# Expert blocks of 121 slots instead of 128, and a gate function that reads the bank directly

## What is computed

```
def expert_block(args):
    xe, e = args
    gu = xe @ w_gate_up[e] + b_gate_up[e]
    gate, up = gu[:, :D_FF], gu[:, D_FF:]
    gate = jnp.minimum(gate, SWIGLU_LIMIT)
    up = jnp.clip(up, -SWIGLU_LIMIT, SWIGLU_LIMIT)
    h = gate * jax.nn.sigmoid(SWIGLU_ALPHA * gate) * (up + 1.0)
    return h @ w_down[e] + b_down[e]
```

## Time and profile before

| | |
|---|---|
| time, median of 3 runs | 1645.02 us (1643.68 to 1648.96) |
| the profiled execution | 1642.78 us, of which the span from first to last instruction is 1641.0 |
| TensorE busy | 1497.4 us, 91% |
| TensorE weight loads | 1177.5 us, 72%, beside the matmuls |
| VectorE busy | 1407.9 us, 86% |
| ScalarE busy | 1011.4 us, 62% |
| GpSimd busy | 156.7 us, 10% |
| granted TensorE clock, mean | 0.955 |
| moved by DMA | 471 MB, 287 GB/s |

### The profile page before, as it was taken

How to read it: one execution, slowest core, us unless ns; L and a number is a source line. 1 busy time by engine, 2 the same in 40 slices (tenths; PEclk the granted TensorE clock), 3 DMA queues, 4 the chain that set the end, 5 groups by cost and what they waited for, 6 DMA issues and landing times. The chain is left out here.

```text
span 1641.0 us, 22871 instructions
## 1 busy us (share of the span) xinstructions
PE 1497.4 (91%) x7059; PEld 1177.5 (72%) x7060; DVE 1407.9 (86%) x1927; ACT 1011.4 (62%) x1201; POOL 156.7 (10%) x196
## 2 busy tenths in 40 slices
PE   5979999939999999999999999999999999999540
PEld 4868753538888888878888888788888888888430
DVE  3964547669999999999999999999999999999538
ACT  4001131137777787777778777777787777777421
POOL 6370001000000000000000000000000000000000
PEclk9979999959999999999999999999999999999775
DMA  8400064127999899889898887888999888989206
GB/s 276 61 1 29 31 218 194 62 91 317 366 376 377 370 368 371 340 341 373 366 371 367 366 367 326 361 370 366 372 371 371 360 338 368 371 369 370 91 16 266
DMA packets 81955, 471.15 MB, mean 287 GB/s; under 512 B 15969, under 2 KB 16965, under 8 KB 64495
## 3 DMA queue, kind: packets, MB, share of 16 engines
q1 hardware_dynamic: 70526, 451.31, 68.6%
q0 software_dynamic: 11232, 19.46, 3.2%
q10 hardware_dynamic: 168, 0.04, 0.0%
HBM read 463.59 MB, written 23.04 MB: 297 GB/s over the span
## 5 line engine op out<-in xcount | busy, mean ns | idle before, releaser
L1463 DVE TENSOR_TENSOR w_lo<-ring_lo,w_hi 128x1024 fp32r<-128x1024 f32 x528 | 616.2, 1218 | 10.9 <-ACT w_hi L1304 5.2
L1304 ACT ACTIVATE w_hi<-ring_lo 128x1024 fp32r<-128x1024 f32 x528 | 537.1, 1056 | 74.0 <-PE bank L1388 55.9
L1388 PE MATMUL bank<-w_hi,x_hi 128*128 128x512 f32 x1056 | 340.2, 403 | 5.6 <-DVE w_lo L1463 3.4
L1388 PE MATMUL bank<-w_lo,x_hi 128*128 128x512 f32 x1056 | 327.6, 392 | 0.0
L1388 PE MATMUL bank<-w_hi,x_lo 128*128 128x512 f32 x1056 | 326.3, 390 | 0.0
L1463 DVE TENSOR_TENSOR w_lo<-w_out,w_hi 128x1024 fp32r<-128x1024 f32 x264 | 310.7, 1218 | 6.2 <-ACT w_hi L1304 6.2
L1304 ACT ACTIVATE w_hi<-w_out 128x1024 fp32r<-128x1024 f32 x264 | 267.1, 1050 | 9.2 <-PE bank L1388 9.2
L1388 PEld LDWEIGHTS bank<-w_lo,x_hi 128*128 128x128 f32 x1056 | 199.2, 189 | 43.0
L1388 PEld LDWEIGHTS bank<-w_hi,x_lo 128*128 128x128 f32 x1056 | 198.8, 188 | 42.9
L1388 PEld LDWEIGHTS bank<-w_hi,x_hi 128*128 128x128 f32 x1056 | 194.5, 189 | 45.0 <-DVE w_lo L1463 3.8
L1388 PE MATMUL bank<-w_hi,h_hi 128*128 128x512 f32 x528 | 175.9, 414 | 0.0
(11 more groups left out here) (317 smaller groups left out, 1399.8 us busy)
## 6 DMA issues: line engine op xcount, KB each, us to landing
ring_lo<-in_w_gate_up SPq DMA_DIRECT2D x132, 2048.0 KB, 10.1
w_out<-in_w_down SPq DMA_DIRECT2D x132, 1024.0 KB, 11.2
ring_lo<-in_w_in SPq DMA_DIRECT2D x4, 2048.0 KB, 22.3
ring_lo<-expert_rows SPq DMA_DIRECT2D x4, 2048.0 KB, 15.2
w_out<-in_w_out SPq DMA_DIRECT2D x2, 2048.0 KB, 8.9
x<-in_x_prompt SPq DMA_DIRECT2D x6, 512.0 KB, 11.7
ffn_in<-hf SPq DMA_DIRECT2D x4, 512.0 KB, 2.6
out_y_p<-of_fin SPq DMA_DIRECT2D x3, 512.0 KB
```

Of the source, the lines that this page charges most:

```text
L1304: nc.scalar.activation(high(j), raw(j), ACT.Copy).then_inc(s["w_hi"], 1)
L1388: last = nc.tensor.matmul(bank[b + u][:], v[:, k, :], part(j)[:, u, :], start=(k == 0 and first), stop=False)
L1463: v.tensor_tensor(low(j), raw(j), high(j).bitcast(F32), ALU.subtract).then_inc(s["w_lo"], 1)
```

## The change

Five things change together:

- A block has `CAP` = 121 slots. The gather and the scatter take 121 rows, the transposes take 121 rows and give 121 columns, the stationary operands `x_hi`, `x_lo`, `h_hi`, `h_lo` have 121 columns (their tiles are packed to 121), and the one-hot operand of the bias has 121. The banks of the transposes keep their step of 128 columns, of which 121 are read (`cols`). The tables count overflow blocks with 121.
- In the router, GpSimd adds 1 to the up part of the bias before VectorE splits it, so the clip of up is between 1 - 7 and 7 + 1 and nothing is added later.
- ScalarE reads the gate from its PSUM bank without the minimum. The function grows with its argument above the limit, so the minimum is taken of its result, against the value at the limit, `GATE_MAX`, in the pass that makes h.
- VectorE's `swiglu` is two passes instead of three.
- TensorE's waits for `gu_read` go; ScalarE waits for the bias matmul (`gu_psum`), and in the second half for the first h, whose buffer it overwrites.

```
+GATE_MAX = LIMIT / (1.0 + math.exp(-ALPHA * LIMIT))
+CAP = 121
+NOVER = ((TOK * TOPK + E * (CAP - 1)) // CAP - E + GROUP) // GROUP * GROUP
...
+            lo, hi = max(FF - h * HB, 0), min(2 * FF - h * HB, HB)
+            if lo < hi:
+                pool.wait_ge(s["bias_in"], 48 * sum(bias_pieces[0:h + 1]))
+                g.tensor_scalar(bf[:, lo:hi], bf[:, lo:hi], 1.0, None, ALU.add).then_inc(s["bias_up"], 1)
...
+            if h in (1, 2):
+                dve.wait_ge(s["bias_up"], h)
...
-        done(v.tensor_scalar(extra, c, float(P), None, ALU.is_gt))
+        done(v.tensor_scalar(extra, c, float(CAP), None, ALU.is_gt))
...
-    x_hi = buf("x_hi", [P, KD, P], F32R)
+    x_hi = buf("x_hi", [P, KD, CAP], F32R)
...
         def gated(q, half):
-            act.wait_ge(s["g_min"], 2 * q + half + 1)
-            nc.scalar.activation(g_sb, g_sb, ACT.Gelu_apprx_sigmoid).then_inc(s["sig"], 1)
+            act.wait_ge(s["gu_psum"], 2 * q + half + 1)
+            if half == 1:
+                act.wait_ge(s["h"], 2 * q + 1)
+            nc.scalar.activation(g_sb[0:CAP], bank[2 * half][0:CAP, :], ACT.Gelu_apprx_sigmoid).then_inc(s["sig"], 1)
...
-                last = nc.tensor.transpose(bank[k // 4][:, (k % 4) * P:(k % 4 + 1) * P], xg[:, k * P:(k + 1) * P], ident[:])
+                last = nc.tensor.transpose(bank[k // 4][:, (k % 4) * P:(k % 4) * P + CAP], xg[0:CAP, k * P:(k + 1) * P], ident[0:CAP, 0:CAP])
...
-                    last = nc.tensor.matmul(bank[b + u][:], v[:, k, :], part(j)[:, u, :], start=(k == 0 and first), stop=False)
+                    last = nc.tensor.matmul(bank[b + u][0:CAP, :], v[:, k, :], part(j)[:, u, :], start=(k == 0 and first), stop=False)
...
-                last = nc.tensor.matmul(bank[b + u][:], tb["pick_row"][:, bass.ds(e, 1)].to_broadcast([96, P]),
+                last = nc.tensor.matmul(bank[b + u][0:CAP, :], tb["pick_row"][:, bass.ds(e, 1)].to_broadcast([96, CAP]),
...
-                if j in (0, 8):
-                    pe.wait_ge(s["gu_read"], 2 * q + j // 8 + 1)
...
             dve.wait_ge(s["gu_psum"], 2 * q + half + 1)
-            g, u = g_sb, u_sb
-            v.tensor_scalar(g, bank[2 * half][:], LIMIT, None, ALU.min).then_inc(s["g_min"], 1)
-            v.tensor_scalar(u, bank[2 * half + 1][:], LIMIT, -LIMIT, ALU.min, ALU.max).then_inc(s["gu_read"], 1)
-            dve.wait_ge(s["gu_read"], 2 * q + half + 3)
+            v.tensor_scalar(u_sb[0:CAP], bank[2 * half + 1][0:CAP, :], LIMIT + 1.0, 1.0 - LIMIT, ALU.min, ALU.max).then_inc(s["clip"], 1)
+            dve.wait_ge(s["clip"], 2 * q + half + 1)
             dve.wait_ge(s["sig"], 2 * q + half + 1)
-            v.scalar_tensor_tensor(out=h_sb, in0=u, scalar=1.0, in1=g, op0=ALU.add, op1=ALU.mult).then_inc(s["h"], 1)
+            v.scalar_tensor_tensor(out=h_sb[0:CAP], in0=g_sb[0:CAP], scalar=GATE_MAX, in1=u_sb[0:CAP], op0=ALU.min, op1=ALU.mult).then_inc(s["h"], 1)
```

More of the change, by code:

```diff
@@ L918, in router @@
     s = {n: sem("r_" + n) for n in (
-        "bias_done consts gffn_in wr_in bias_in sq sums rows mix_var mix_root mm x_new xsq x_var x_root hf hfT_psum hfT logits "
+        "bias_done bias_up consts gffn_in wr_in bias_in sq sums rows mix_var mix_root mm x_new xsq x_var x_root hf hfT_psum hfT logits "
         "sub exp mask rank_psum step pool_step done tabs".split())}
@@ L1171, in _ @@
         done(v.tensor_copy(c, bank[7][:, NT * E:(NT + 1) * E]))
-        done(v.tensor_scalar(extra, c, float(P), None, ALU.is_gt))
-        for t in range(2, NT):
-            done(v.scalar_tensor_tensor(out=extra, in0=c, scalar=float(t * P), in1=extra, op0=ALU.is_gt, op1=ALU.add))
+        done(v.tensor_scalar(extra, c, float(CAP), None, ALU.is_gt))
+        for t in range(2, -(-TOK // CAP)):
+            done(v.scalar_tensor_tensor(out=extra, in0=c, scalar=float(t * CAP), in1=extra, op0=ALU.is_gt, op1=ALU.add))
         done(v.tensor_tensor_scan(upto, ones[:, 0:E], extra, 0.0, ALU.mult, ALU.add))
@@ L1183, in _ @@
         done(v.tensor_tensor(of[:, 2, :], b_no, of[:, 1, :], ALU.subtract))
-        v.tensor_scalar(tb["over_base"][:], of[:, 2, :], 1.0, float(P), ALU.add, ALU.mult)
+        v.tensor_scalar(tb["over_base"][:], of[:, 2, :], 1.0, float(CAP), ALU.add, ALU.mult)
         v.tensor_scalar(tb["over_i"][:, 0, :], of[:, 0, :], float(E - 1), None, ALU.min)
@@ L1201, in experts @@
     w_lo = buf("w_lo", [P, SLOTS, 1024], F32R)
-    x_hi = buf("x_hi", [P, KD, P], F32R)
-    x_lo = buf("x_lo", [P, KD, P], F32R)
-    h_hi = buf("h_hi", [P, KD, P], F32R)
-    h_lo = buf("h_lo", [P, KD, P], F32R)
+    x_hi = buf("x_hi", [P, KD, CAP], F32R)
+    x_lo = buf("x_lo", [P, KD, CAP], F32R)
+    h_hi = buf("h_hi", [P, KD, CAP], F32R)
+    h_lo = buf("h_lo", [P, KD, CAP], F32R)
     yflat = mid["ymix"][:, :, :].rearrange("p m t -> p (m t)")
@@ L1217, in experts, with cols @@
     s = {n: sem("e_" + n) for n in (
-        "w_hi w_lo w_used onehot sel_psum sel idx x_in xT_psum x_hi x_lo gu_psum gu_read g_min sig h hT_psum h_hi h_lo "
+        "w_hi w_lo w_used onehot sel_psum sel idx x_in xT_psum x_hi x_lo gu_psum clip sig h zeroed hT_psum h_hi h_lo "
         "y_psum y_sb y_stored y_out y_free curd turns".split())}
     block = stack.enter_context(nc.Block())
+    def cols(b):
+        return b[:].rearrange("p (k t) -> p k t", k=4)[:, :, 0:CAP]
     gu = ring_lo[:, :, :].rearrange("p (k u) (f n) -> p k u f n", k=KD, f=2)
@@ L1272, in gather @@
             pool.sem_inc(s["turns"], 1)
-            nc.gpsimd.indirect_dma_start(xg, None, scratch["hf"], bass.IndirectOffsetOnAxis(ap=idx_next[:, 0:1].bitcast(U32), axis=0),
+            nc.gpsimd.indirect_dma_start(xg[0:CAP], None, scratch["hf"], bass.IndirectOffsetOnAxis(ap=idx_next[0:CAP, 0:1].bitcast(U32), axis=0),
                                          bounds_check=TOK - 1, oob_is_err=False).then_inc(s["x_in"], 16)
@@ L1338, in body @@
             for h in range(2):
-                last = nc.scalar.activation(yo[:, h * 512:(h + 1) * 512], bank[4 + h][:], ACT.Copy, scale=gate_cur[:, 0:1])
+                last = nc.scalar.activation(yo[0:CAP, h * 512:(h + 1) * 512], bank[4 + h][0:CAP, :], ACT.Copy, scale=gate_cur[0:CAP, 0:1])
             last.then_inc(s["y_sb"], 1)
@@ L1378, in h_transposes @@
             for k in range(4):
-                last = nc.tensor.transpose(bank[6 + half][:, k * P:(k + 1) * P], h_sb[:, k * P:(k + 1) * P], ident[:])
+                last = nc.tensor.transpose(bank[6 + half][:, k * P:k * P + CAP], h_sb[0:CAP, k * P:(k + 1) * P], ident[0:CAP, 0:CAP])
             last.then_inc(s["hT_psum"], 1)
@@ L1468, in take_x @@
                 c = slice(4 * h, 4 * h + 4)
-                last = v.tensor_tensor(x_lo[:, c, :].rearrange("p k t -> p (k t)"), bank[h][:],
-                                       x_hi[:, c, :].rearrange("p k t -> p (k t)").bitcast(F32), ALU.subtract)
+                last = v.tensor_tensor(x_lo[:, c, :], cols(bank[h]), x_hi[:, c, :].bitcast(F32), ALU.subtract)
             last.then_inc(s["x_lo"], 1)
@@ L1517, in over @@
             body(b + E, 0, False)
-        v.memset(zero[:], 0.0).then_inc(s["gu_read"], 2)
-        dve.wait_ge(s["gu_read"], 2)
+        v.memset(zero[:], 0.0).then_inc(s["zeroed"], 1)
+        dve.wait_ge(s["zeroed"], 1)
         pick(0, zero[:, 0:1])
```

11 lines of the change are left out of this document (4 added, 7 removed).

## The result

The change makes the kernel slower: a median of 1671.57 us against 1644.35 of the kernel before on the same chip, ratio 1.0161 with a 95% interval of 1.0134 to 1.0188. The forecast was 1618 us with a range of 1590 to 1650, and the time lies above it. The profiled execution has a span of 1667.5 us, 26.5 more than before.

The account below looks back on a forecast made before the run. The prediction took TensorE's instruction stream, 33 blocks of 36.19 us, to bound the kernel. It summed -28.0 (products' loads), -1.2 (exposed loads) and +2.1 (bias loads) to -27.1 us, giving 1618 us from 1645.0, range 1590 to 1650.

Parts of the forecast that it names:

- 0.2265 us: TensorE's expert blocks: distance between back-to-back products, 13 ns over the 0.2133 us stream; 144 make 32.6 of 36.19 us.
- (a): Products at half clock: two take 0.85 us, the bare stream, so the surplus isn't a number of TensorE's cycles.
- (b): Bias matmul against product, both 512 columns: bf16 recorded at 378 ns, product at 389, so 11 ns of waiting in each.
- (c): Products' weight load: starts with the product before, lasts 188 ns, next product starts 38 ns after its end; 188 + 38 = 226.
- The test that the prediction named: Products in the profile after: if the load falls to 182 ns and the distance stays 226, the load wasn't the chain.
- -28.0: Products with 121 stationary columns: each load 5.9 ns shorter, 0.85 us a block over 33 blocks, -28.0 us.
- The exposed loads (-1.2): First loads after selection, transposes or bias, six a block: each 5.9 ns shorter, -1.2 us in all.
- +2.1: Bias matmuls with 121 columns: exposed loads rise from 98 to 140 ns or not, 4.2 us or 0; middle taken.
- Part 2: VectorE's minimum on the gate goes, bias plus one is stored: 1.2 us a block off VectorE, worth 0, hidden by TensorE.
- Rival 3: Products' loads slower with 484-byte slices and no full width, from 189 ns up: 1675 us; chance 0.13 shared with another rival.
- Rival 2: Products: 121 columns do nothing, the 13 ns are of the moving side; 1646 us; chance 0.32.
- Rival 1: Products: the whole surplus goes, loads shrinking faster than 0.84 ns a column, -50.8 us; 1595 us; chance 0.19.

Follow-up runs that it names:

- e1: The changed kernel with CAP back at 128, so two VectorE passes and stored bias plus one alone: 1643.39 us, ratio 0.9999 to the kernel before.
- e9: e1 with each product and bias matmul streaming 448 of its 512 columns, loads unchanged: 1571.07 us.
- e10: e1 with products and bias matmuls using 64 of the 128 stationary columns, transposes full: 1676.24 us.
- e15: e1 with the four stationary tiles starting 32 bytes further on, slices still 512 bytes apart: 1668.66 us.
- e5: The changed kernel with 121-column slices laid out 512 bytes apart and gather and scatter of 128 rows: 1647.10 us, ratio 1.0018.
- e4: The changed kernel with gather and scatter of 128 rows, all else at 121: 1661.49 us, ratio 1.0103.
- e2: The changed kernel with the old three VectorE passes, old waits and no stored bias plus one: 1714.84 us, ratio 1.0438.
- e11: e2 with gather and scatter of 128 rows: 1660.30 us, ratio 1.01.
- e14: e1 with the four stationary tiles starting 4, 8, 12 and 16 bytes off their old places, slices still 512 bytes apart: 1665.86 us.
- e17: e1 with the four stationary tiles starting 128 bytes further on, slices still 512 bytes apart: 1666.05 us.
- e6: e1, full 128 columns, with the slices of the x and h tiles 516 bytes apart: 1665.01 us.
- e3: The changed kernel with 121-column slices laid out 512 bytes apart, DMAs still of 121 rows: 1664.82 us, ratio 1.0124.

## Why the prediction was wrong, point by point

**What bounds the kernel.** Right. TensorE's stream does: VectorE relieved changes nothing (e1), a shorter stream takes 73 us off (e9).

**What sets 0.2265 us.** Observations (a) and (b) stand as rows; that the surplus belongs to the 4-byte operands was not tested by itself. Step (c) failed. That 188 + 38 makes 226 was read as a chain, but the next product doesn't wait for the load's end; how long the load lasts is hidden: 182 ns with 232 between products (after), 134 with 229.8 (e10), 188 with 202.6 (e9), 188 with 233.3 (e15). The test that the prediction named, the distance staying while the load falls, came out in a stronger form.

**The term -28.0.** The slope was right: 188 to 182 ns is 6, against 5.9 in the sum, and 134 at 64 columns lies on it. Its way onto the path was wrong. In place of -28.0 the products cost +0.61 us a block, 20 us over 33 blocks, of which e5, whose slices stand right, keeps 0.15 a block, 5 us. So the layout makes three quarters of it (e4 against e5: 14.4 us), and the width by itself 5 us; with the gains below taken off, an ordinary block of e5 is 0.05 us longer than one of e1, 1.5 us in all.

**The small terms.** The transposes were put at 0 and gain 0.07 us a block, 103 ns from start to start instead of 109. Their moving side shrinks to 121 columns as well, which may be why; it wasn't tested. The exposed loads (-1.2) are not to be told from the products' new unevenness. The bias load goes to 134 ns, near the upper end of the range given for it (140). The Trainium skill ("TensorE: Matmul & The Clock Gate", Weight-path perf modes) has the fast load only at 128 weights; the trace agrees here (98 ns with 128, 134 with 121). But no time came of it: the six bias matmuls take 924 instead of 955 ns a block, -1.0 us in all where +2.1 stood. It is the mistake of (c) once more, a load priced that is covered.

**The missing term.** The prediction counts the gathers (33) and says of the tail that the change doesn't touch it. The two indirect DMAs, whose row count the change alters, stand in its sum with nothing, and without a reason. Their cost is 10.1 us in the changed kernel and some 15.5 beside products at the old distance. The trace of before showed half of it: a cover of 13.7 us for a landing of 11.2. What 121 rows do to the landing stood in no row, and asked for a range of its own.

**Part 2.** The 0 is right at 128 slots (e1) and for the reason given. The sentence on what would happen without it, VectorE's 35.0 beside TensorE's 35.4, looked at the wrong thing: with 121 slots it is worth 43 us (e2), not because VectorE has less to do but because it reaches the indices 0.7 us earlier. Once the gather is in time again it is worth nothing (e11: 1660.3, e4: 1661.5). The bias plus one is hidden: with it the first x transposes come 0.2 us later (358.9 against 358.7), less than they differ between kernels of the same front, and e1 is no slower.

**The rivals.** Rival 3 named the packed slices, forecast 1675 us and comes near by its size. Its mechanism was refuted by its own condition: it decided from a load of 189 ns up, and the load is 182. That it came near is an accident of a mirrored price; of the 28 us that the changed kernel loses against e1, none are the loads', 14.4 are the layout's and 10.1 the DMAs'. Rival 2 had the distance follow the moving side, as e9 bears out, and let it be untouched by the change, which it wasn't. Rival 1, with a narrower load freeing the stream, is refuted by e10.

**What stays open.** Why the relative place matters was not shown. The distances after a pause run through a pattern (before, in a run of 24: 236, 224, 231, 236, 228, 232, then 227 from about the tenth on; e15: 235 and 232 in turn, to the end of the run), which looks as if the reads of slice and stream settle into a rhythm that fits or doesn't. That is a reading, not a result. How coarse the grid is beyond 128 bytes isn't known, and 512 is known only from the kernels that stand on it. Nor is it known why 120 and 64 columns in slices that stand right give 233.3 and 229.8 ns, and why 121 gives now 226.7 and now 231.

## What to carry to other kernels

Two durations that add up to the distance are no chain: before a load is put on the path, find a row where it is shorter or the stream is, and see if the distance follows. When a tile's size changes, go through everything that takes its shape: the row count of its DMAs, and the place of its slices relative to what is read beside them. An engine with time to spare can still hold the start of a transfer with none; price the transfer's cover, not the engine's share.

## What the runs showed of the hardware

With fp32r operands, back-to-back products of 512 columns take 226.67 ns when each 128-column stationary slice starts a multiple of 512 bytes away from the streamed buffers, and 232.0 to 233.3 ns when the slices are 4 to 128 bytes off (e14 to e17) or 516 bytes apart (e6), with loads of 188 ns in both cases. In this kernel that is 20 to 25 us of 1644. With 121 columns in slices that stand right they take either 226.7 or 231 ns, block by block (e3, e5). An indirect DMA of 121 rows takes 192 packets where 128 rows take 144 and 112 rows 128, and a gather of them lands 3.2 us later for the same bytes.
